# Streaming encoder step: the eight gates of the first branch ahead, its eight projections in the local attention

## Chip, core and metric

The kernel runs on one core of one Trainium2 chip. The time is what the device needs for one execution, in microseconds (us). TensorE does the matrix products; ScalarE, VectorE and GpSimd work beside it, and SyncE starts most of the DMA transfers. In the rows they are PE, ACT, DVE, POOL and SP; PEld is TensorE's loading of weights.

## What is computed

Two layers of a hybrid encoder, over 640 tokens (512 of a prompt, 128 of eight samples), width 1024. From the reference, cut:

```python
def token_mix(h, pos, lw, rel_bias, cache):
    qa, ka, va, ub, cq, ckv, kpe, ud, gate_in = split_cols(h @ lw['w_in'])
    ...   # o_a: window attention, o_b: pooling mixer, o_c: latent attention
    o_d, new_conv = conv_module(ud, conv_hist, lw['conv_w'], lw['conv_b'], lw['conv_ln_g'], lw['conv_ln_b'])
    gates = jax.nn.sigmoid(gate_in.reshape(B, T, BRANCHES, D_MODEL))
    merged = (gates[:, :, 0] * (o_a @ lw['w_o_a']) + gates[:, :, 1] * (o_b @ lw['w_o_b'])
              + gates[:, :, 2] * (o_c @ lw['w_o_c']) + gates[:, :, 3] * (o_d @ lw['w_o_d']))
    return merged @ lw['w_out'], ...
```

`conv_module` is a gated causal convolution of 31 taps, a layer norm over its 512 channels and a SiLU. After the mixers comes a feed-forward part (SwiGLU).

## The kernel before

Activations lie with the 128 features of a tile on the partitions and the 640 tokens along the free axis, in two halves of 320. Weights come in units of 128 output features: a wide unit has eight 128x128 tiles (512 KB), a projection unit four (256 KB). Each fp32 product is done in three passes over rounded parts (`w_hi*h_hi`, `w_hi*h_lo`, `w_lo*h_hi`), so one tile costs six matmuls of 320 columns: 48 for a wide unit, 24 for a projection unit.

There is no scheduler: each engine has its program written out by hand, and semaphores with counts tie them together. Units go through two slots. Unit n lies in slot n % 2 and, of the units touched here, its result in the PSUM pair `G[n % 2]`. SyncE loads `w_raw` when the unit two earlier has been split; GpSimd splits it (first the 384 columns of tiles 0 to 2, then the rest) when TensorE has finished the matching part of the unit two earlier; TensorE multiplies when it is split and when `G` has been read (`g_free`).

A layer begins with 22 wide units of the input projection. VectorE meanwhile runs the convolution. After them TensorE does small fp32 work for the branches, in the banks 4 to 7:

- `lnm`: sum over the channels of the convolution's output (L711)
- `pool` (g = 0 to 3): the pooling mixer's products (L732), each waiting for VectorE's `pooled`
- `ckvn`, `lnv`, `cqn`: sums of squares (L711) of the latent keys, of the centred convolution output and of the latent queries. ScalarE writes the squares (`squares`, L1149), then takes the root (`stds`, L1154), VectorE the reciprocal (L1613) and the scaling. From `lnv` come the layer norm, SiLU (L1310), `o_hi` (L1313) and `o_lo` (L1801), which is the input of branch D's projections; from `cqn` come the scaled queries (L1806)
- `kpe`: a product (L746) of the rotary keys `kper`, which VectorE rotates (L1814) and signals as `kpe_rot`
- transposes of new rows (`new`, `vwin`), and then the local attention, ten blocks `j`. In each, TensorE does the scores of the block after (`a_scores`), a transposition of the probabilities (`a_turn`) that VectorE has normed (`a_back`), and the values (`a_values`) after ScalarE's copy (L1359)

Between these pieces stand the 32 merges, eight of each branch in the order D, B, A, C. A merge is a gate unit from `h` in `G[0]`, its sigmoid on ScalarE into `sg` (`merge_gate`), a projection unit from `o` in `G[1]`, and the product on VectorE, which goes into `macc` (the first branch) or is added to it (`merge`). `macc` lies where `x` was; `x` is parked in HBM meanwhile. The merges of branch D were 0 and 1 before the attention, and 2 to 7 in the blocks j = 0 to 2, two in each; from j = 3 on branches B and A follow. Later, the latent attention's last part, for the samples (L978 to L998), has only one weight tile of a gate between short products.

ScalarE's functions lie in tables, and another function (root, sigmoid, SiLU, exponential) may need an ACT_TABLE_LOAD; a copy or a square needs none.

Of the kernel before, what the change touches and what calls it, by code (L numbers as in the profile page):

```python
# [16 lines left out]
ACT = mybir.ActivationFunctionType  # L17
ALU = mybir.AluOpType
# [174 lines left out]
def encoder(nc, io):  # L193
    ctx = ExitStack()
    with ctx:
# [271 lines left out]
        def a_merges(j):  # L467

            return (2 + 2 * j, 3 + 2 * j) if j < 4 else (6 + j,)
# [49 lines left out]
        def _(eng):  # L519
# [6 lines left out]
            for l in range(L):  # L526
# [64 lines left out]
        def _(eng):  # L591
            eng.sem_inc(w_split.sem, w_split.credit)
            eng.sem_inc(lo_plain.sem, lo_plain.credit)
            for l in range(L):
# [20 lines left out]
                pairs(A_UNITS // 2, M_PAIRS, UW, 4 * P)  # L615
# [9 lines left out]
        def _(eng):  # L625
# [43 lines left out]
            for l in range(L):  # L669
# [34 lines left out]

                def colsum(name, tiles, waits, square=None):
                    for n, tile in enumerate(tiles):
                        waits(n)
                        for hf, cols in halves:
                            if n == 0:
                                fill(l, (name, hf))  # L710
                            mm = eng.matmul(B[4 + hf][:, 0:HALF], ones[:, :], tile[:, cols],  # L711
                                            start=(n == 0), stop=(n == len(tiles) - 1))
                            if n == len(tiles) - 1:
                                mm.then_inc(side.sem, 1)
                        if square is not None and n < len(tiles) - 1:
                            mm.then_inc(sq_used.sem, 1)
# [31 lines left out]

                eng.wait_ge(ckv_ready.sem, ckv_ready.at(l, 1))
# [381 lines left out]
        def _(eng):  # L1131
# [42 lines left out]
            for l in range(L):  # L1174
# [100 lines left out]

                eng.wait_ge(hist_out.sem, hist_out.at(l, 16 * 4))

                for g in range(4):
                    gain = vec[:, V_PSC + g:V_PSC + g + 1]
# [8 lines left out]
                merge_gate(0)  # L1288
# [3 lines left out]
                stds(l, lambda hf: ("ckvn", hf), P)  # L1292

# [11 lines left out]
                eng.dma_start(out("o_ckv"), ckvT[:, :]).then_inc(outs.sem, 16)  # L1305

# [9 lines left out]
                merge_gate(1)  # L1316
# [31 lines left out]

                a_exps(0)
                for j in range(10):  # L1350
# [4 lines left out]
                    if n[0] == KT:  # L1355
                        branch_high(BRANCH_B, pool_out, pool_out_s)
                    merge_gate(n[0])
# [242 lines left out]
        def _(eng):  # L1600
# [33 lines left out]
            for l in range(L):  # L1634
# [141 lines left out]
                def merge(n, m, first=False):  # L1776
# [4 lines left out]

                    if not isinstance(n, int) or n:
                        eng.wait_ge(merged.sem, merged.at(l, n))
                    acc = macc[:, bass.ds(m, 1), :].rearrange("p a t -> p (a t)")
                    if first:
                        for hf, cols in halves:
                            ins = eng.tensor_tensor(acc[:, cols], sg[:, cols], G[1][:, hf, 0:HALF], ALU.mult)
                            ins.then_inc(g_free[1].sem, 1)
                        eng.wait_ge(g_free[1].sem, g_free[1].at(l, n * 2 + (A_UNITS + 2)))
                        eng.sem_inc(merged.sem, 1)  # L1790
                        return
# [16 lines left out]

                eng.wait_ge(x_parked.sem, x_parked.at(l, 16))
                merge(0, 0, first=True)  # L1810


# [5 lines left out]
                merge(1, 1, first=True)  # L1818
# [47 lines left out]
                for j in range(10):  # L1866
                    if j + 1 < 10:
                        a_front(j + 1)
                    a_back(j)
                    for n in a_merges(j):  # L1870
                        if n == KT:
                            branch_low(BRANCH_B, pool_out, pool_out_s)
                        merge(n, n % KT, first=n < KT)
# [425 lines left out]
```

## Time and profile before

| | before |
|---|---|
| median of 3 runs | 2490.18 us (2490.05 to 2490.38) |
| the profiled execution's own time | 2506.54 us |
| its span, first to last instruction | 2504.7 us |
| PE busy | 2376.0 us, 95% |
| DVE, POOL, ACT busy | 1291.9, 953.3, 860.1 us |
| mean granted TensorE clock | 0.970 |

The profiled execution took 16.36 us more than the median of the runs. Its span is 1.84 us less than its own time. A busy TensorE says nothing of its speed: the granted clock is shown apart, 1.00 for 2.4 GHz and 0.50 for 1.2 GHz.

### The profile page before, as it was taken

How to read it: one execution, taken by the hardware profiler on the slowest of the kernel's cores; microseconds unless marked ns; L12 is line 12 of the kernel's file. 1: busy time of each engine (PE TensorE's matmuls, PEld its weight loads, DVE VectorE, ACT ScalarE, POOL GpSimd, SP SyncE). 2: the span in 40 equal slices, each digit the busy share in tenths (PEclk: the TensorE clock that was granted, in tenths of full speed). 3: DMA queues.
4: the chain of work that ended last, by engine and by line, in shares of the span. 5: the costliest groups of instructions: out<-in, count | busy, mean ns of one | idle time of the engine just before them, and what ended most of it. 6: DMA issues, size and time to landing. Idle time of an engine off the chain costs nothing.

```text
span 2504.7 us, 40008 instructions
## 1 busy us (share of the span) xinstructions
PE 2376.0 (95%) x15160; PEld 2220.4 (89%) x15160; DVE 1291.9 (52%) x2296; ACT 860.1 (34%) x1688; POOL 953.3 (38%) x988
## 2 busy tenths in 40 slices
PE   6997999999999899999979989999999999999996
PEld 5996998777899899999979969987779999999996
DVE  6976243333225953826479752433332378366374
ACT  2014233334212553625410142333333145345252
POOL 3551454222166233332445415532224642423231
PEclk9999999999699999999989989999999999999998
DMA  5341121011023122222234311211012322222121
GB/s 173 113 129 52 55 73 55 26 39 39 19 97 121 51 93 70 84 92 68 69 114 139 107 32 64 68 51 38 27 38 64 113 76 75 86 76 93 61 88 55
DMA packets 70131, 186.78 MB, mean 75 GB/s; under 512 B 19648, under 2 KB 22304, under 8 KB 68960
## 3 DMA queue, kind: packets, MB, share of 16 engines
q1 hardware_dynamic: 53280, 162.23, 20.1%
q10 hardware_dynamic: 16704, 22.52, 2.7%
q8 instruction: 101, 1.65, 0.3%
q14 instruction: 46, 0.38, 0.0%
HBM read 172.41 MB, written 14.14 MB: 74 GB/s over the span
## 4 chain that ended last, share of the span: by engine, by line
PE 89%; DVE 6%; issue 2%; ACT 1%; ACTq 0%; DMA 0%; SPq 0%; DVEq 0%
PE gemm L641 44%; PE gemm L1057 16%; PE gemm L1047 13%; PE side L1057 3%; PE side L909 2%; PE side L930 2%; PE side L860 1%; DVE rstd L1613 1%; PE side L910 1%; PE side L790 1%; DVE act_lo L2038 1%; PE side L869 1%; PE side L917 1%; DVE prod L1642 1%; PE side L711 1%
## 5 line engine op out<-in xcount | busy, mean ns | idle before, releaser
L604 POOL CAST w_hi<-w_raw 128x384 fp32r<-128x384 f32 x376 | 213.0, 566 | 895.8 <-PE gemm L641 874.6
L621 POOL TENSOR_TENSOR ring_lo<-w_raw,ring_hi 128x512 fp32r<-128x512 f32 x232 | 307.9, 1330 | 590.3 <-ACT ring_hi L1475 590.3
L606 POOL TENSOR_TENSOR w_lo<-w_raw,w_hi 128x384 fp32r<-128x384 f32 x376 | 435.7, 1159 | 30.1
L641 PE MATMUL gemm<-h_hi,w_hi 128*128 128x320 f32 x1728 | 423.1, 326 | 20.1 <-DVE h_lo L1619 16.8
L641 PE MATMUL gemm<-h_lo,w_hi 128*128 128x320 f32 x1728 | 398.5, 312 | 0.0
L641 PE MATMUL gemm<-h_hi,w_lo 128*128 128x320 f32 x1728 | 398.1, 312 | 0.0
L641 PEld LDWEIGHTS gemm<-h_hi,w_hi 128*128 128x128 f32 x1728 | 290.4, 191 | 49.7 <-issue 36.3
L1057 PE MATMUL gemm<-act_hi,ring_hi 128*128 128x320 f32 x960 | 299.4, 312 | 19.0 <-issue 9.9
L1057 PE MATMUL gemm<-act_lo,ring_hi 128*128 128x320 f32 x960 | 298.7, 311 | 0.0
L1057 PE MATMUL gemm<-act_hi,ring_lo 128*128 128x320 f32 x960 | 298.4, 311 | 0.0
L641 PEld LDWEIGHTS gemm<-h_lo,w_hi 128*128 128x128 f32 x1728 | 294.1, 191 | 0.0
L641 PEld LDWEIGHTS gemm<-h_hi,w_lo 128*128 128x128 f32 x1728 | 293.1, 191 | 0.0
L1475 ACT ACTIVATE ring_hi<-w_raw 128x512 fp32r<-128x512 f32 (+1 forms) x272 | 167.6, 618 | 244.8 <-PE gemm L1047 201.7
L1793 DVE TENSOR_TENSOR prod<-gate,gemm 128x320 f32<-128x320 f32 x96 | 42.5, 484 | 326.2 <-PE gemm L641 326.2
L1057 PEld LDWEIGHTS gemm<-act_hi,ring_hi 128*128 128x128 f32 x960 | 182.2, 190 | 20.7 <-issue 20.7
L1057 PEld LDWEIGHTS gemm<-act_lo,ring_hi 128*128 128x128 f32 x960 | 182.5, 190 | 0.0
L1057 PEld LDWEIGHTS gemm<-act_hi,ring_lo 128*128 128x128 f32 x960 | 182.5, 190 | 0.0
L1696 DVE SCALAR_TENSOR_TENSOR side<-conv_prompt,vec,side 128x512 f32<-128x512 f32 x232 | 174.2, 751 | 0.0
L2115 DVE TENSOR_TENSOR x<-gemm,x 128x320 f32<-128x320 f32 x96 | 42.7, 486 | 224.6 <-PE gemm L1047 224.6
L1047 PE MATMUL gemm<-hu_hi,ring_hi 128*128 128x320 f32 x640 | 146.1, 309 | 0.0
L1047 PE MATMUL gemm<-hu_hi,ring_lo 128*128 128x320 f32 x640 | 145.8, 309 | 0.0
L1047 PE MATMUL gemm<-hu_lo,ring_hi 128*128 128x320 f32 x640 | 145.7, 309 | 0.0
(280 smaller groups left out, 4247.0 us busy)
## 6 DMA issues: line engine op xcount, KB each, us to landing
w_raw<-in_ws_ff SPq DMA_DIRECT2D x120, 512.0 KB, 3.2
w_raw<-in_ws_gate SPq DMA_DIRECT2D x64, 512.0 KB, 3.3
w_raw<-in_ws_in SPq DMA_DIRECT2D x44, 512.0 KB, 3.3
w_raw<-in_ws_proj SPq DMA_DIRECT2D x64, 256.0 KB, 2.6
w_raw<-in_ws_out SPq DMA_DIRECT2D x16, 512.0 KB, 3.3
w_raw<-in_ws_fd SPq DMA_DIRECT2D x16, 384.0 KB, 3.0
x_park<-x ACTq DMA_DIRECT2D x2, 2560.0 KB, 12.1
x<-x_park ACTq DMA_DIRECT2D x4, 1280.0 KB, 5.8
```

The costliest lines, as they stand in the source:

```text
L604: eng.tensor_copy(w_hi[s][:, cols], w_raw[s][:, cols]).then_inc(w_high.sem, 1)
L606: eng.tensor_tensor(w_lo[s][:, cols], w_raw[s][:, cols], w_hi[s][:, cols].bitcast(F32), ALU.subtract).then_inc(w_split.sem, 1)
L621: eng.tensor_tensor(lo, src, hi.bitcast(F32), ALU.subtract).then_inc(lo_plain.sem, 1)
L641: mm = eng.matmul(dst[:, hf, 0:HALF], w, r[:, k, cols], start=first and k == 0 and part == 0, stop=last and k == kk - 1 and part == 2)
L909: eng.matmul(bank[:, 0:w], qh[h % 2][:, P * i:w], kh[h % 2][:, 0:w], start=True, stop=False)
L930: mm = eng.matmul(B[6][part, i * P:(i + 1) * P], v_tok[k][:, 64 * h:64 * h + 64], PT[i % 2][:, k * P:(k + 1) * P], start=(k == 0), stop=(k ...
L1047: mm = eng.matmul(dst[:, hf, 0:HALF], w[:, cut], r[:, cols], start=part == 0 and k == 0 and t == 0, stop=part == 1 and k == tiles - 1 and ...
L1057: mm = eng.matmul(dst, w[:, cut], r[act][:, k, :], start=fresh and k == 0 and t == 0, stop=k == 3 and t == 2, skip_group_check=not fresh)
L1475: eng.activation(hi, src, ACT.Copy).then_inc(op_high.sem, 1)
L1696: eng.scalar_tensor_tensor(acc, src, w, acc, ALU.mult, ALU.add).then_inc(conv_step.sem, 1)
L1793: eng.tensor_tensor(t2[0][:, cols], sg[:, cols], G[1][:, hf, 0:HALF], ALU.mult)\
L2115: eng.tensor_tensor(x[:, m, cols], G[u % 2][:, hf, 0:HALF], x[:, m, cols], ALU.add)\
```

## The change

Branch D's eight gate units come first, one after the other: gate 0 behind `lnm`, gates 1 and 2 in halves behind the four pooling products, gate 3 behind `ckvn`, 4 behind `lnv`, 5 behind `cqn`, 6 behind `kpe`, 7 behind the transposes. ScalarE writes each sigmoid straight into `macc`. The eight projection units then stand in the attention: 0 to 2 in block 0, 3 to 5 in block 1, 6 and 7 in block 2; VectorE multiplies `macc` by each in place. The other branches are as they were. Since both kinds of unit now come in runs, gate m and projection m lie in slot and `G` m % 2. The loads and the splits follow that order. The core of the diff:

```diff
         def a_merges(j):
-            return (2 + 2 * j, 3 + 2 * j) if j < 4 else (6 + j,)
+            return () if j < 3 else ((KT, KT + 1) if j == 3 else (KT - 2 + j,))
+        def a_projections(j):
+            return range(3 * j, min(3 * j + 3, KT)) if j < 3 else ()
...
+                with eng.Fori(0, KT // 2) as i:
+                    for s in range(2):
+                        unit(i * 2 + (A_UNITS + s), s, layer_of(io["ws_gate"], l * M_PAIRS + i * 2 + s), UW)
+                with eng.Fori(0, KT // 2) as i:
+                    for s in range(2):
+                        unit(i * 2 + (A_UNITS + KT + s), s, layer_of(io["ws_proj"], l * M_PAIRS + i * 2 + s), 4 * P)
...
-                merge_units(0, KT + 5)
+                merge_units(KT, KT + 5)
...
+                def first_gate(m, first=0, last=KT):
+                    if first == 0:
+                        psum(m % 2, A_UNITS // 2 + m // 2)
+                    for t in range(first, last):
+                        product(l, A_UNITS + m, G[m % 2], m % 2, t, KT, h_hi, h_lo)
+                def first_projection(m):
+                    psum(m % 2, A_UNITS // 2 + KT // 2 + m // 2)
+                    for t in range(4):
+                        if m == 0:
+                            eng.wait_ge(o_split.sem, o_split.at(l, t + 1))
+                        product(l, A_UNITS + KT + m, G[m % 2], m % 2, t, 4, o_hi, o_lo)
...
+                first_gate(0)
                 for g in range(4):
...
-                    merge_tiles(0, 2 * g, 2 * g + 2)
+                    first_gate(1 + g // 2, 4 * (g % 2), 4 * (g % 2) + 4)
                 colsum("ckvn", *sq_tiles(0, 1), square=True)
+                first_gate(3)
                 colsum("lnv", *sq_tiles(1, 4), square=True)
+                first_gate(4)
                 colsum("cqn", *sq_tiles(5, 2), square=True)
-                merge_tiles(0, 8, 12)
-                merge_tiles(1, 0, 12)
-                eng.wait_ge(loaded, 16 * 5)
+                first_gate(5)
                 eng.wait_ge(kpe_rot.sem, kpe_rot.at(l, 1))
...
+                first_gate(6)
                 eng.wait_ge(ckv_ready.sem, ckv_ready.at(l, 1))
...
+                first_gate(7)
                 a_scores(0)
...
-                    merge_tiles(n[0], 0, 8)
+                    for m in a_projections(j)[:2]:
+                        first_projection(m)
+                    if n:
+                        merge_tiles(n[0], 0, 8)
                     a_turn(j)
-                    merge_tiles(n[0], 8, 12)
+                    for m in a_projections(j)[2:]:
+                        first_projection(m)
+                    if n:
+                        merge_tiles(n[0], 8, 12)
                     a_values(j)
```

On ScalarE:

```diff
+                def first_gate(m):
+                    eng.wait_ge(unit_done.sem, unit_done.at(l, A_UNITS + m + 1))
+                    for hf, cols in halves:
+                        eng.activation(macc[:, m, cols], G[m % 2][:, hf, 0:HALF], ACT.Sigmoid)\
+                           .then_inc(g_free[m % 2].sem, 1)
```

On VectorE:

```diff
-                eng.wait_ge(x_parked.sem, x_parked.at(l, 16))
-                merge(0, 0, first=True)
...
-                merge(1, 1, first=True)
+                def first_merge(m):
+                    eng.wait_ge(unit_done.sem, unit_done.at(l, A_UNITS + KT + m + 1))
+                    for hf, cols in halves:
+                        eng.tensor_tensor(macc[:, m, cols], macc[:, m, cols], G[m % 2][:, hf, 0:HALF], ALU.mult)\
+                           .then_inc(g_free[m % 2].sem, 1)
...
                     a_back(j)
+                    for m in a_projections(j):
+                        first_merge(m)
```

On TensorE, around `kpe` in the first layer, before (the last tile of merge 1's projection, the two products, the first transposes):

```order
L641 MATMUL gemm<-o_hi,w_hi_57 128x320
L641 MATMUL gemm<-o_lo,w_hi_57 128x320 x2
L641 MATMUL gemm<-o_hi,w_lo_58 128x320 x2
L746 MATMUL side<-kpe_raw,dup 128x320 [waits side_read6,kpe_rotated,consts_loaded]
L746 MATMUL side<-kpe_raw,dup 128x320 [waits side_read7]
L756 MATMUL side<-ident,ckv 16x128 [waits side_read5,gemm_read1,ckv_ready]
L757 MATMUL side<-ident,v_window 16x128
```

The same place now (the last tile of gate 5, the two products, the first of gate 6):

```order
L653 MATMUL gemm<-h_hi,w_hi_57 128x320 x2
L653 MATMUL gemm<-h_lo,w_hi_57 128x320 x2
L653 MATMUL gemm<-h_hi,w_lo_58 128x320 x2
L773 MATMUL side<-kpe_raw,dup 128x320 [waits side_read6,kpe_rotated]
L773 MATMUL side<-kpe_raw,dup 128x320 [waits side_read7]
L653 MATMUL gemm<-h_hi,w_hi_53 128x320 [waits w_split,gemm_read0]
L653 MATMUL gemm<-h_hi,w_hi_53 128x320
```

The product stays where it was among the small ones, but a gate instead of merge 0's projection and merge 1 stands between `cqn` and it, and a gate behind it. On ScalarE, between the layer norm's root and the squares of `cq`, before:

```order
L1154 ACTIVATE rstd<-side,eps 128x320 [waits side_filled,ckv_ready]
L1154 ACTIVATE rstd<-side,eps 128x320 [waits side_filled]
L1305 DMA o_ckv<-ckv 128x640
L1149 ACTIVATE square_77<-cq 128x640 [waits gemm_read0]
L1149 ACTIVATE square_76<-cq 128x640 [waits gemm_read1]
L1310 ACT_TABLE_LOAD
L1310 ACTIVATE conv_out<-conv_out,vec 128x640 [waits ln_scaled]
```

and now:

```order
L1189 ACT_TABLE_LOAD [waits side_filled]
L1189 ACTIVATE rstd<-side,eps 128x320 [waits ckv_ready]
L1189 ACTIVATE rstd<-side,eps 128x320 [waits side_filled]
L1353 DMA o_ckv<-ckv 128x640
L1315 ACT_TABLE_LOAD
L1315 ACTIVATE x<-gemm 128x320 [waits unit_done]
L1315 ACTIVATE x<-gemm 128x320
L1184 ACTIVATE square_77<-cq 128x640 [waits gemm_read0]
L1184 ACTIVATE square_76<-cq 128x640 [waits gemm_read1]
L1359 ACT_TABLE_LOAD
L1359 ACTIVATE conv_out<-conv_out,vec 128x640 [waits ln_scaled]
```

Gate 4's sigmoid (into `x`, that is `macc`) with a table load stands ahead of the squares, so they and the SiLU wait for gate 4's unit.

## Rows read from the trace of the kernel before

**Rows 1.** Windows: us, busy of PE, PEld, DVE, ACT, POOL, clock, DMA share, GB/s

```profile
185.12:325.27 140.15, 125.42 (x739) 110.82 (x737) 59.24 (x100) 48.80 (x86) 48.96 (x66) 0.94 0.18 56
1427.53:1567.67 140.14, 125.40 (x738) 110.81 (x736) 59.34 (x100) 48.85 (x86) 48.98 (x66) 0.94 0.19 56
```

**Rows 2.** PE's waits between 180 and 262 us: total, times, longest

```profile
PE gemm L641 <- issue: 5.3, 1, 5.3
PE side L711 <- ACT square L1149: 4.6, 3, 1.6
PE side L732 <- DVE rstd L1746: 2.7, 2, 2.2
PE side L790 <- ACT v_sample L1329: 1.4, 1, 1.4
```

**Rows 3.** Timeline of PE: start, us, what, idle before

```profile
216.35 2.42 PE L711 MATMUL side<-square,ones 128*128 128x320 f32 x8 [1.56 <-ACT square L1149]
...
224.06 0.87 PE L641 MATMUL gemm<-o_hi,w_hi 128*128 128x320 f32 x2 [5.30 <-issue]
```

**Rows 4.** Windows of 4 us around the longest wait, columns as in rows 1

```profile
218.00:222.00 4.00, 0.77 (x3) 0.19 (x1) 3.96 (x4) 1.31 (x3) 0.00 (x0) 0.92 0.00 0
222.00:226.00 4.00, 1.94 (x7) 1.97 (x8) 3.30 (x5) 3.94 (x6) 0.00 (x0) 0.50 0.00 0
```

**Rows 5.** The chain, in order of time, in attention block 1

```profile
277.29 7.24 PE gemm L641 x48
...
284.96 3.52 PE gemm L641 x24
```

**Rows 6.** Timeline of ACT, sigmoid of gate 0 to the root of `cqn`

```profile
205.86 0.77 ACT L1266 ACTIVATE gate<-gemm 128x320 f32<-128x320 f32 x2 [1.08 <-PE gemm L641]
...
215.56 1.36 ACT L1149 ACTIVATE square<-cq 128x640 f32<-128x640 f32 x2
216.94 1.28 ACT L1310 ACT_TABLE_LOAD   x1
220.88 0.83 ACT L1310 ACTIVATE conv_out<-conv_out,vec 128x640 f32<-128x640 f32 x1 [2.66 <-DVE conv_out L1765]
...
226.95 1.28 ACT L1154 ACT_TABLE_LOAD   x1
228.25 0.95 ACT L1154 ACTIVATE rstd<-side,eps 128x320 f32<-128x320 f32 x2
...
285.21 0.60 ACT L1359 ACTIVATE rstd<-side 128x512 f32<-128x512 f32 x1
```

**Rows 7.** Timeline of DVE: queries, rotation, and block 2's front to block 1's norm

```profile
229.29 4.15 DVE L1613 RECIPROCAL rstd<-rstd 128x640 f32<-128x640 f32 x1 [1.50 <-ACT rstd L1154]
233.48 2.11 DVE L1806 SCALAR_TENSOR_TENSOR cq<-cq,vec,rstd 128x640 f32<-128x640 f32 x2
...
236.52 0.82 DVE L1814 TENSOR_TENSOR kpe_raw<-kpe_raw,cos_sin 64x640 f32<-64x640 f32 x1
...
277.32 0.69 DVE L1833 SCALAR_TENSOR_TENSOR square<-side,bias_prompt 128x512 f32<-128x512 f32 x1 [0.58 <-PE side L790]
...
281.06 1.39 DVE L1862 TENSOR_TENSOR square<-square,softmax_stats 128x512 f32<-128x512 f32 x1
```

**Rows 8.** Windows: latent attention of the samples, both layers, columns as in rows 1

```profile
617.16:671.26 54.10, 50.52 (x197) 40.91 (x197) 9.33 (x38) 13.72 (x48) 6.00 (x8) 0.56 0.08 25
...
1859.50:1895.40 35.90, 32.31 (x196) 25.71 (x195) 9.33 (x38) 13.72 (x48) 6.00 (x8) 0.98 0.12 37
```

**Rows 9.** Timeline of POOL: one wide unit's split, in the input projection

```profile
178.41 0.72 POOL L604 CAST w_hi<-w_raw 128x640 fp32r<-128x640 f32 x1 [2.56 <-PE gemm L641]
179.21 1.58 POOL L606 TENSOR_TENSOR w_lo<-w_raw,w_hi 128x640 fp32r<-128x640 f32 x1
181.05 0.50 POOL L604 CAST w_hi<-w_raw 128x384 fp32r<-128x384 f32 x1 [0.27 <-PE gemm L641]
181.63 1.02 POOL L606 TENSOR_TENSOR w_lo<-w_raw,w_hi 128x384 fp32r<-128x384 f32 x1
```

More of the change, by code:

```diff
@@ L614, in _ @@
                 pairs(0, A_UNITS // 2, UW, UW)
-                pairs(A_UNITS // 2, M_PAIRS, UW, 4 * P)
+                pairs(A_UNITS // 2, KT // 2, UW, UW)
+                pairs(A_UNITS // 2 + KT // 2, KT // 2, 4 * P, 4 * P)
+                pairs(A_UNITS // 2 + KT, M_PAIRS - KT, UW, 4 * P)
                 pairs(A_UNITS // 2 + M_PAIRS, KT // 2, UW, UW)
@@ L1273, in branch_high @@
                         eng.activation(o_hi[:, t, NP:T], sample(t), ACT.Copy).then_inc(o_high.sem, 1)
+                def first_gate(m):
[3 more added lines that the diff above has]
+                           .then_inc(g_free[m % 2].sem, 1)
+                eng.wait_ge(x_parked.sem, x_parked.at(l, 16))
+                first_gate(0)
                 eng.wait_ge(hist_out.sem, hist_out.at(l, 16 * 4))
                 for g in range(4):
+                    if g == 2:
+                        first_gate(1)
                     gain = vec[:, V_PSC + g:V_PSC + g + 1]
@@ L1286, in _ @@
                        .then_inc(freed(("pool", g, 1)), 1)
-                merge_gate(0)
+                first_gate(2)
                 eng.wait_ge(pooled.sem, pooled.at(l, 4))
@@ L1292, in _ @@
                 stds(l, lambda hf: ("ckvn", hf), P)
+                first_gate(3)
                 def centred(k):
@@ L1305, in _ @@
                 eng.dma_start(out("o_ckv"), ckvT[:, :]).then_inc(outs.sem, 16)
+                first_gate(4)
                 squares(l, 2, lambda k: cq[:, k, :], 5, lambda k: read_unit(eng, l, 14 + k))
@@ L1315, in _ @@
                 stds(l, lambda hf: ("cqn", hf), 2 * P)
-                merge_gate(1)
+                first_gate(5)
+                first_gate(6)
                 for hf, cols in halves:
@@ L1347, in a_exps @@
                     eng.activation(stat(j, 4), stat(j, 4), ACT.Exp).then_inc(a_esink.sem, 1)
+                first_gate(7)
                 a_exps(0)
@@ L1354, in _ @@
                     n = a_merges(j)
-                    if n[0] == KT:
+                    if j == 3:
                         branch_high(BRANCH_B, pool_out, pool_out_s)
-                    merge_gate(n[0])
+                    if n:
+                        merge_gate(n[0])
                     bank = filled(eng, l, ("At", j))
@@ L1774, in branch_low, with merge @@
                            .then_inc(o_split.sem, 1)
-                def merge(n, m, first=False):
+                def merge(n, m):
                     eng.wait_ge(unit_done.sem, unit_done.at(l, n * 2 + (A_UNITS + 2)))
                     eng.wait_ge(g_free[0].sem, g_free[0].at(l, n * 2 + (A_UNITS + 2)))
-                    if not isinstance(n, int) or n:
-                        eng.wait_ge(merged.sem, merged.at(l, n))
+                    eng.wait_ge(merged.sem, merged.at(l, n))
                     acc = macc[:, bass.ds(m, 1), :].rearrange("p a t -> p (a t)")
[L1785 to L1791, printed above, removed]
                     for hf, cols in halves:
@@ L1817, in _ @@
                 eng.memset(mask_q[:, 0:CHUNK], 1.0).then_inc(masks.sem, 1)
-                merge(1, 1, first=True)
+                def first_merge(m):
[3 more added lines that the diff above has]
+                           .then_inc(g_free[m % 2].sem, 1)
+                    eng.wait_ge(g_free[m % 2].sem, g_free[m % 2].at(l, 2 * (A_UNITS // 2 + KT // 2 + m // 2) + 2))
+                    eng.sem_inc(merged.sem, 1)
                 def a_front(j):
@@ L1872, in _ @@
                             branch_low(BRANCH_B, pool_out, pool_out_s)
-                        merge(n, n % KT, first=n < KT)
+                        merge(n, n % KT)
                 branch_low(BRANCH_A, window_out, window_out_s)
```

## The prediction

> **What bounds the kernel now.** I read the page first: TensorE is busy for 95% of the span, so matrix work sets most of the time and only two things can be won, its waits and its half-speed stretches. Then the windows by stage. The change touches the stretch from `lnm` to branch B's first gate; it takes 140.15 us in the first layer and 140.14 in the second, and TensorE is busy for only 125.4 of them, at a mean granted clock of 0.94 [rows 1]. The reader should see that the two layers are the same, so one timeline does for both. Next the list of TensorE's waits there: 5.3 once, 4.6 in three times, 2.7 in two and 1.4 once, together 14.0 us [rows 2]. The timeline says what each is. The 5.3 stands before the first `gemm<-o_hi`: merge 0's projection waits for the layer norm, SiLU and the split of the convolution's output [rows 3]. The list calls it "issue", but the instruction behind it reads `o_hi` and `o_lo`. The 4.6 are the waits for ScalarE's squares, one each for `ckvn`, `lnv` and `cqn`, the last 1.56 [rows 2, 3]. The 2.7 are pooling products that wait for VectorE, the 1.4 the first scores, which wait for ScalarE to clear the last transposes [rows 2].
>
> Then the clock. A mean of 0.94 over 140.15 us is about 17 us at 1.2 GHz (0.06 x 2 x 140.15) [rows 1]. Around the longest wait it falls shortly before 222 (0.92 in one window, 0.50 in the next) [rows 4]; the work resumes at 224.06 [rows 3], so some 2.7 us of the 17 lie in the wait and cost nothing. In the other 14 TensorE works at half speed and loses 7.0 us. So one layer's stretch holds 119.1 us of work at full speed and 21.0 us of loss. The work stays: the same tiles are multiplied. Nothing before or behind the stretch is moved.
>
> **The change, part by part.** Gate units: 7.24 us each behind a small product [rows 5], 7.04 of it (48/24 of the 3.52 that a projection unit takes [rows 5]) for the matmuls alone. They need only `h` and weights.
>
> *Pooling waits, 2.7 us.* Each pooling product now has half a gate, 3.5 us, behind it instead of two tiles, 1.8 us. The wait in question was at most 2.2 us long [rows 2] with 1.8 us of cover, so VectorE needs no more than 4.0 us between two products plus what ScalarE adds. But it computes its levels without waiting for TensorE, and only the last step, about 1.3 us, needs the product before. Gate 0, another 7 us, has let it get ahead. I take all 2.7 off. ScalarE's new sigmoids, 0.77 [rows 6], stand before the copies that free banks; half a gate covers them.
>
> *Squares, 4.6 us.* They stay. In the new order `ckvn`, `lnv` and `cqn` each stand right behind a gate, and on ScalarE the squares stand behind that gate's sigmoid, as `ckv`'s square did before. Sigmoid 0.77 and one square, half of 1.36 [rows 6], make 1.45; the three old waits average 1.53 [rows 2]. I keep 4.6.
>
> *The 5.3 us.* Branch D's projections now stand in the attention, over 30 us later. Gone.
>
> *The 1.4 us before the scores.* Gate 7, 7 us, covers ScalarE's copies. Gone.
>
> *The new wait.* `kpe` needs `kpe_rot`, and VectorE's rotation stands behind the norm of `cq`. Before, two projections and a gate ran in between and nobody waited for it. Take the end of gate 4 as zero. ScalarE: sigmoid and two squares of `cq`, 0.77 + 1.36, with their overlap until 2.05; table load 1.28, until 3.35; from the first SiLU to the next table load 226.95 - 220.88 = 6.07, until 9.4; that load and the root, 226.95 to 229.20, until 11.7 [rows 6]. The 2.66 us for which ScalarE waited before the first SiLU [rows 6] are gone: the layer norm's root, reciprocal and scaling (1.28 + 0.95, 4.15, about 3.3) start when `lnv` ends, a gate earlier, at -7.1, and end at 2.6. VectorE: reciprocal and scaling, 229.29 to 235.59, 6.3, until 18.1; rotation 0.82, until 18.9 [rows 7]. TensorE: wait 1.5, `cqn` 2.42 [rows 3], gate 5 7.1, done at 11.0. So it waits 7.9 us, in each layer. Queued behind it are gate 6, which needs nothing of it, and the transposes. This takes back more than the 5.3 gave.
>
> *Table loads.* Between the sigmoids stand new loads. Those for gates 3 and 4 lie under gates; the two on the path just worked out are in its sum at 1.28 us, as the row shows. The load begins at 216.94, when the squares end at 216.92, so nothing lies ahead of it [rows 6].
> The Trainium skill (ScalarE: Activation LUTs, "What ACT_TABLE_LOAD costs") counts about 2.66 us for every switch, a load of 1.28 and a drain of 1.38. By it, with the drain beside a load already in the row, the wait would be 10.7 us instead of 7.9, and the whole time 5.5 us longer than my sum; this trace agrees with the load and shows no drain.
>
> *Projections in the attention.* In block 1 TensorE has two projections, 7.04 us, between the scores and the turn; VectorE needs from 277.32 to 282.45, 5.1 us, for the front of one block and the norm of the other [rows 7], and 0.9 for a product that frees `G`. Covered, by 1 us. Block 2 has no third projection, so its values stand right behind the turn and wait for ScalarE's copy, 0.60 [rows 6], with its start about 0.9 us. A bound: 0.6 to 1.1.
>
> *Weights.* GpSimd's split of a wide unit is 0.72 + 1.58 + 0.50 + 1.02 = 3.82 us [rows 9] against 7.04 of TensorE. A projection unit has 1.52 of it for the first three tiles and a fourth tile, bounded by nothing and by the 2.30 of five tiles [rows 9]: 1.5 to 3.8 us against 3.52. At the upper end it costs 0.3 a unit, 2.4 a layer; by columns it is near 2.0 and costs nothing, which I take.
>
> *Clock.* No row shows the new order, so two bounds. Below: nothing is lost. Above: 7.0 us as now. Of the three old half-speed stretches the first followed a pooling wait, the last the transposes and the 1.4 us; both causes go, gates follow at once. After the 7.9 us wait I expect what followed the 5.3: work resumed at 224.06 and reached full speed near 228.3, 4.3 us at half speed, 2.2 lost.
>
> Sum for a layer: 4.6 + 7.9 + 0.9 + 2.2 = 15.6 us of loss for 21.0, a gain of 5.4; for two 10.8. Against the profiled execution's own 2506.54 us that is 2495.7. But this execution is no plain copy of the timed runs. In the first layer the samples' attention, the same instructions, took 54.10 us at a clock of 0.56, in the second 35.90 at 0.98 [rows 8]: 18.2 us. Without that the execution would have its own time at 2488.3, close to the median of 2490.18 and 1.8 below; so the timed runs, alike within 0.33 us, seem free of it. The gain is taken off the median: 2490.2 - 10.8 = **2479.4 us**.
>
> **Rivals.**
> *A. The clock falls as much as now.* The squares' waits break the gates and the new wait is longer than the old. Then 13.4 + 7.0 = 20.4 us for 21.0: 1.2 us gained, 2489.0, the same within what counts. For it: the old pooling wait of 2.2 us was followed by half speed. Against it: dense units between the waits. Chance 0.12. Partial forms lie between 2480 and 2489.
>
> *B. The samples' attention falls to half speed in the timed runs.* Everything behind the stretch starts 5 us earlier in layer one and 11 in layer two, and that stage, one tile of a gate between short fp32 products, is where the clock fell in one layer of two. Its price, 18.2 us [rows 8], is more than the gain: 2497.6, slower. It decides as soon as one layer has it in most runs. Against it: three timed runs of the old kernel do not show it. Chance 0.11.
>
> *C. The table switch costs its drain.* The mechanism here would be an idle gap of 1.4 us by each of two loads on the path to `kpe_rot`, in both layers, against the 0.02 us between square and load that the row shows. 2484.9, chance 0.03.
> It is the rule of the Trainium skill's page ScalarE: Activation LUTs that is weighed above.
>
> *D. The gates hide nothing more than they did:* the wait moves whole, that is the `kpe` wait is longer than the waits removed. From 5.3 + 2.7 + 1.4 = 9.4 us saved, 8.8 are given back (7.9 + 0.9). So without the clock almost nothing is won: 0.6 a layer. That is A seen from the waits, 2489.0, and its chance is in A's 0.12. My forecast hangs on the half-speed stretches, 4.8 of the 5.4 us.
>
> **How the numbers follow.** My own case, chance 0.74, runs from 2475.0 (no half speed: 7.6 us a layer) to about 2486 (a clock loss of 5). With C it is faster, 0.77. A gives the same, 0.12; B slower, 0.11. 0.2%, some 5 us, is about what a measurement of this kernel can tell from no change. The range 2473 to 2491 takes in my case, A and C with a little beyond the best, and leaves out B.
>
> **What the changed kernel's profile would show.** No wait before a `gemm<-o_hi` of branch D and none at the first scores. One wait of about 8 us at the `kpe` products, released by VectorE's rotation, in both layers. Three waits of 1.5 us for squares. From `lnm` to branch B's first gate 134.7 us by my sum, 132.5 if nothing runs at half speed; a mean clock there of 0.96 or more. Attention blocks 0 to 2 without a wait but the 0.9 us. I am wrong if GpSimd's splits or VectorE's products of the projections make TensorE wait in blocks 0 to 2, if the clock stays down for more than some 5 us, or if the samples' attention takes near 54 us in the runs that are timed.

## The result, and the profile after

The change made the kernel slower. This kernel's median is 2507.07 us over 20 runs (2488.64 to 3339.57), that of before is 2492.07 over 20 (2490.05 to 2531.13), the three runs of the table ahead of the prediction among them. The ratio is 1.0048, 95% interval 1.0026 to 1.0071: 0.48% slower, where 0.4% faster was forecast. The run of 3339.57 us, at a mean clock of 0.65, is left out below.

A median hides here what the single runs show. Each kernel's times fall into levels 15 to 21 us apart, and the profiles, which caught runs on all three, say what a level is: the number of layers in which the samples' latent attention ran at half speed. A run without a profile is put on a level by its time. Over this comparison and those of the experiments the old kernel had 119 runs, the new one 31:

| runs (median, us) | no layer | one layer | two layers |
|---|---|---|---|
| before, 119 runs | 66 (2491.5) | 39 (2508.8) | 14 (2529.5) |
| after, 31 runs | 1 (2488.6) | 22 (2506.7) | 8 (2521.6) |

Level by level the new kernel is 2 to 8 us faster. It is slower because 30 of its 31 runs have at least one such layer, and of the old kernel's 53 of 119.

The profiled execution of after took 2504.89 us, with this span and clock (a digit for each fortieth of the span):

```profile
span 2503.0 us, 39978 instructions
...
PEclk9999999999999899999999999999978999999998
```

The 7 and 8 at three quarters of the span are the samples' attention of layer 2. Windows over that stage in both layers and, above them, from `lnm` to branch B's first gate (us, busy of PE, PEld, DVE, ACT, POOL, clock, DMA share, GB/s), the stretches of [rows 1] and [rows 8]:

```profile
185.54:325.35 139.81, 123.26 (x738) 109.13 (x736) 65.59 (x100) 44.89 (x83) 51.71 (x66) 0.95 0.19 55
1409.62:1547.79 138.17, 121.62 (x740) 107.79 (x738) 65.57 (x100) 44.88 (x83) 51.72 (x66) 0.96 0.19 56
617.24:653.41 36.17, 32.59 (x198) 26.02 (x197) 9.33 (x38) 13.70 (x48) 6.00 (x8) 0.97 0.12 37
1839.67:1893.96 54.29, 50.70 (x198) 41.23 (x197) 9.34 (x38) 13.70 (x48) 5.99 (x8) 0.56 0.08 25
```

Two things are to be read. The changed stretch, 140.15 and 140.14 us before [rows 1], is now 139.81 and 138.17: a gain of 0.34 + 1.97 = 2.3 us, by one execution of each, where 10.8 were forecast. And the stage that wasn't touched costs 54.29 - 36.17 = 18.1 us more in layer 2 than in layer 1, as it did in layer 1 of before [rows 8]. The two profiled executions have one such layer each, so their difference, 2506.54 to 2504.89, tells nothing of the loss in the medians.

TensorE's waits between 183 and 330 us (total, times, longest), to be laid beside [rows 2]:

```profile
PE side L773 <- DVE kpe_raw L1853: 7.5, 1, 7.5
PE side L738 <- ACT square L1184: 4.4, 3, 1.5
PE side L760 <- DVE rstd L1798: 3.2, 1, 3.2
PE side L848 <- ACT prod L1411: 0.7, 1, 0.7
```

They sum to 15.8 us, before to 14.0. Layer 2 has the same four. The waits of 5.3 and 1.4 us are gone, the one for `kpe_rot` has come, and the pooling wait, of which nothing was to be left, has grown. With the prediction's estimate of 119.1 us of work, 139.81 - 119.1 - 15.8 = 4.9 us went to half speed in layer 1 and 3.3 in layer 2. The chain of after shows where, first a pooling product and its half gate in layer 1 and in layer 2, then the `kpe` product and gate 6 in layer 1 (start, us):

```profile
214.00 1.97 PE side L760 x4
215.97 4.49 PE gemm L653 x24
...
1438.43 1.34 PE side L760 x4
1439.77 3.54 PE gemm L653 x24
...
261.86 2.50 PE side L773 x4
264.36 9.43 PE gemm L653 x48
```

The same product and half gate take 6.46 us in layer 1 and 4.88 in layer 2: 1.6 us of half speed behind the pooling wait. A gate is 7.04 us [rows 5] and took 9.43, and `kpe` 2.50 instead of about 1.3: 3.6 us of half speed behind the new wait. Windows of 4 us, ahead of the end of that wait and behind it, show the clock:

```profile
256.00:260.00 4.00, 0.00 (x0) 0.00 (x0) 3.96 (x2) 1.17 (x3) 0.84 (x1) 0.87 0.18 66
...
264.00:268.00 4.00, 4.00 (x15) 3.71 (x15) 0.00 (x0) 0.00 (x0) 0.00 (x0) 0.50 0.00 0
```

### The profile page after: what moved, and what is told of

Read it like the earlier page. It is cut to its first block, busy times and chain, and to the rows that moved or that the text cites. A ratio compares the mean times of both kernels' runs of the same rounds, so it can differ in the third digit from the quotient of the medians.

```text
span 2503.0 us, 39978 instructions
## 1 busy us (share of the span) xinstructions
PE 2370.0 (95%) x15160; PEld 2215.4 (89%) x15160; DVE 1307.1 (52%) x2296; ACT 851.9 (34%) x1682; POOL 957.3 (38%) x988
## 4 chain that ended last, share of the span: by engine, by line
PE 89%; DVE 7%; ACT 2%; issue 2%; ACTq 0%; DMA 0%; SPq 0%; DVEq 0%
PE gemm L653 43%; PE gemm L1092 16%; PE gemm L1082 13%; PE side L1092 3%; PE side L944 2%; PE side L965 2%; PE side L895 1%; DVE rstd L1665 1%; PE side L945 1%; DVE act_lo L2087 1%; PE side L738 1%; PE side L818 1%; PE side L904 1%; PE side L952 1%; DVE prod L1694 1%
```

## The experiments

Three questions: do the half-speed layers make the loss (the first seven runs), what do the two waits cost (three), and is a version to be had that beats both (two). In the diffs `-` and `+` are against the changed kernel unless it is said.

### Is the loss in the levels, and does the start time move them?

My theory: what decides is when the samples' attention starts. Its start in layer 1 is the same in both kernels, 617.16 and 617.24 us [rows 8]. In layer 2 it starts at 1839.67 now; before it was 1859.50 [rows 8], less the 18.2 that the half-speed layer had added 1841.3. So the new kernel is 1.6 us earlier there. The rival: the levels are luck of the day, and the new kernel has its share of runs without a fall like the old.

The first run gives those 1.6 us back with work that nobody needs: in layer 2, eleven products into `G[0]`, whose result the gate behind them overwrites, ahead of merge 11. (Merge 11 is the fourth of branch B, in attention block 5; the text put on record ahead of the run calls it branch A's gate.)

```
                         if t % KT == 0:
                             psum(t // KT, n + A_UNITS // 2)
+                        if n == 11 and t == 0 and l in (1,):
+                            eng.wait_ge(w_split.sem, w_split.at(l, unit * 2 + 1))
+                            for _ in range(11):
+                                eng.matmul(G[0][:, 0, 0:HALF], w_hi[0][:, 0:P], h_hi[:, 0, 0:HALF],
+                                           start=True, stop=True)
```

> The changed kernel with 11 extra matmuls of 320 columns (h_hi by a weight tile that is loaded, their result overwritten) ahead of branch A's gate 11 in the second layer alone: 1.6 us of delay for everything behind, nothing else changed. Theory S (start time): whether the samples' attention falls to half speed is set by the time at which it starts, to about a us; the new order made it start 1.6 us sooner in the second layer than an undisturbed run of the old kernel does (1839.7 against 1859.5 - 18.2 = 1841.3), and at the same time in the first. Then the delay takes most of the falls away: median about 2490.2 (2488.6 + 1.6). Rival T (the order itself, or what it leaves behind, makes the fall likely): 1.6 us do nothing, median about 2508.7. Rival N (pure chance for each run): a mixture as before, most runs at 2507.

12 runs, median 2506.17: five without a half-speed layer (2488.3 to 2491.1), five with one, two with two. Ratio to before 1.0013 (0.9975 to 1.0050). With more work five runs of twelve are on a level that the kernel without it reached once in 31; but the median of 2490.2 that my theory gave didn't come. The same was then tried on the kernel before (twelve products, layer 2), where a theory of start times wants a clear change: eight runs of 12 with none, four with one, median 2493.73, ratio 0.9998 (0.9964 to 1.0032). Beside it the plain old kernel had 17 of 35 with none; twelve runs can't tell that from no change.

The changed kernel again, unchanged:

> The changed kernel itself once more, beside fresh runs of the old one. Level theory: each kernel has levels some 17.5 us apart, by how many of its two layers fall to half speed in the samples' attention (old 2490.5, 2508.5, 2530; new 2488.6, 2506.5, 2522), and which level a run takes is decided outside the kernel, differently from job to job. Then both kernels take all levels, in like shares, and level by level the new one is 2 us faster. Order theory: the new order makes the fall likely; at least 9 of 12 runs at 2505 or above, against half or fewer of the old kernel's.

12 runs, median 2506.95, ratio 1.0053 (1.0013 to 1.0093): none without, seven with one, five with two. The rival falls: the old kernel beside it had 17 of 29 without. This run's profile has its half-speed layer in layer 1, whose start the change hardly moved. So the 1.6 us in layer 2 can't be the whole reason. Nor does the start alone, to half a us, tell the outcome. The first score product of layer 1, in this execution and in that of after:

```profile
619.79 0.38 PE L1013 MATMUL side<-ckv_cache_t,q_latent_sample 128*128 128x128 f32 x2
```

```profile
620.25 0.38 PE L1013 MATMUL side<-ckv_cache_t,q_latent_sample 128*128 128x128 f32 x2
```

The same kernel, 0.46 us apart at this point, is at half speed in that stage the first time and at full speed the second.

The first run again, and the same products in layer 1 instead of 2 (`l in (0,)`):

> The same kernel as e1 once more: the changed kernel with 1.6 us of extra matmuls in the second layer alone, ahead of branch A's gate 11. In e1 5 of 12 runs had no fall to half speed in the samples' attention, in the changed kernel itself 1 of 31. If the start time of the stage matters: again 4 to 8 of 12 runs at 2488 to 2492. If e1 was chance: at most one.

> The changed kernel with the same 1.6 us in the first layer alone; both layers' stages then start 1.6 us later. If the start time matters for each layer, the shares change here too, and differently from e1 and e9, where only the second was moved: I expect 3 to 8 of 12 runs without a fall. If only the distance between the two layers' stages matters, it is as in the changed kernel: at most one.

With the shift in layer 2: median 2506.13, three without, six with one, three with two; ratio 1.0005 (0.9970 to 1.0040). That is under the four to eight that I expected, but with the first run 8 of 24 against 1 of 31. With the shift in layer 1: median 2490.78, seven without, four with one, one with two; ratio 0.9995 (0.9955 to 1.0035). So 1.6 us of useless work in layer 1 bring the median back by 16 us; in layer 2 they leave it where it was. That such work changes the share is shown: the old kernel beside these runs kept its usual one (17 of 35 and 14 of 24 without). That it does so by the start time is the likely reading, and isn't shown. Against a simple rule speaks that two edits below, gate 6 ahead of `kpe` and gate 2 whole, start the samples' attention earlier by 6 to 20 us in their traces and leave the share as it was: 2 and 0 runs of 12 without.

### What if the stage is made denser?

In the samples' attention a tile of merge 24's gate, the first of branch C, is multiplied for each sample, the first of them behind the scores of two samples. Now each tile stands one sample earlier, the first ahead of the loop behind the first scores, and the last sample has none. In all nine half-speed stages that the profiles caught, the clock falls 3.1 to 4.2 us behind the first score product; now one dense tile lies ahead of that place and one on it. First on the kernel before, then on the changed one:

```
                 s_scores(0)
+                merge_tiles(3 * KT, 0, 1)
                 for b in range(NB):
...
-                    merge_tiles(3 * KT, b, b + 1)
+                    if b + 1 < NB:
+                        merge_tiles(3 * KT, b + 1, b + 2)
```

> The kernel before the change; in the samples' attention the first weight tile of the gate stands between the scores of sample 0 and 1 (before: behind both), every later tile one sample earlier, none at sample 7. Nothing is added or left out. In all falls and most no-falls seen, the clock falls 3.3 to 4.1 us behind the stage's first product or not at all, so what TensorE does in the first 4 us of the stage would decide. If that is so: with two tiles of dense work there and no wait, no run falls: all at 2490 to 2494. If the whole stage is too thin and the first 4 us are not special: the falls come at other places, as often.

> The changed kernel with the same shift of the gate's tiles. If the start of the stage decides: all runs at 2488 to 2492, the changed kernel's lowest level, and about 2 us under the old kernel with the same shift. If not: levels as in the changed kernel itself.

Before with it: all 12 runs between 2489.2 and 2495.2, median 2492.41, ratio 0.9958 (0.9920 to 0.9996). After with it: all 12 between 2485.1 and 2491.3, median 2487.43, ratio 0.9949 (0.9915 to 0.9983). Windows of the latter over the stage in both layers:

```profile
616.97:653.18 36.21, 32.58 (x197) 25.97 (x197) 9.80 (x38) 13.73 (x48) 6.01 (x8) 0.98 0.12 37
...
1839.71:1875.92 36.21, 32.58 (x196) 25.93 (x197) 9.81 (x38) 13.72 (x48) 6.01 (x8) 1.00 0.12 37
```

Full speed in both, in 36.21 us, while the start in layer 2 is the same 1839.7 as in the profile of after. Eight tiles, each moved by one sample, make the new kernel 19.5 us faster than itself (2487.43 to 2506.95) and faster than the old one. It settles the sign: without the half-speed layers the change is worth 2492.41 - 2487.43 = 5.0 us, and the loss comes whole from the stage that it doesn't touch. The stretch from `lnm` to branch B's first gate explains these 5.0 us, in both layers, first in the old order with the moved tiles, then in the new:

```profile
185.90:328.04 142.14, 125.80 (x739) 111.45 (x737) 59.55 (x100) 48.80 (x86) 49.59 (x66) 0.94 0.19 55
1413.12:1553.58 140.46, 125.70 (x739) 111.33 (x737) 59.54 (x100) 48.86 (x86) 48.98 (x66) 0.94 0.19 55
```

```profile
185.42:325.32 139.90, 123.37 (x739) 109.28 (x737) 65.58 (x100) 44.91 (x83) 51.79 (x66) 0.95 0.19 55
1409.83:1547.76 137.93, 121.40 (x739) 107.56 (x737) 65.56 (x100) 44.91 (x83) 51.79 (x66) 0.96 0.19 56
```

282.6 against 277.8 us is 4.8 of the 5.0. The 2.3 us read further up are smaller because the old order's stretch isn't the same in every execution: its layer 1 took 140.15 us in the profile of before and 142.14 here, where the pooling waits are 4.4 us instead of 2.7.

### What do the new waits cost?

`kpe`: gate 6 ahead of the product that waits.

```
                 first_gate(5)
+                first_gate(6)

                 eng.wait_ge(kpe_rot.sem, kpe_rot.at(l, 1))
...
-                first_gate(6)
                 eng.wait_ge(ckv_ready.sem, ckv_ready.at(l, 1))
```

> The changed kernel with gate 6 ahead of the kpe product instead of behind it. The wait for the rotation was 7.5 us, and behind it TensorE worked 7.3 us at half speed (3.6 lost). If the wait is the step that took the gain back: gate 6 covers 7.0 of it, at most 0.5 is left, the half-speed piece goes; 10.6 us a layer, 21 in all: 2467.5 in runs without a fall in the samples' attention, 2485.7 with one. If TensorE meets another wait in its place (the transposes behind it need banks that ScalarE clears after gate 6's sigmoid): less than 10 in all.

12 runs, median 2485.27: eight between 2483.2 and 2487.6, the level with one half-speed layer, two above (2502.5 and 2504.5, two layers by the profile of the former), two below (2462.96 and 2470.04). Ratio 0.9941 (0.9910 to 0.9971). Level by level 21.4 us under the changed kernel, for the level with one. Waits between 183 and 340 us, and the clock behind:

```profile
PE side L760 <- DVE rstd L1798: 3.2, 1, 3.2
...
PE side L774 <- DVE kpe_raw L1853: 0.5, 1, 0.5
```

```profile
260.00:280.00 20.00, 19.23 (x124) 15.03 (x124) 4.82 (x13) 7.67 (x16) 3.11 (x6) 1.00 0.11 31
```

The wait is down from 7.5 to 0.5 us and the half speed behind it is gone, clock 1.00. Two waits of 7.0 less, and half speed of 3.6 us in layer 1 and 3.2 in layer 2 (gate 6 took 9.04 us there), make 20.8 of the 21.4 measured. A gate's order, nothing else.

Pooling: all of gate 2 between the third and the fourth pooling product, and none of it behind the fourth.

```
-                    first_gate(1 + g // 2, 4 * (g % 2), 4 * (g % 2) + 4)
+                    if g < 2:
+                        first_gate(1, 4 * g, 4 * g + 4)
+                    elif g == 2:
+                        first_gate(2)
```

> The changed kernel with all of gate 2 between the pooling products 2 and 3, none behind 3. The wait for pooled of group 3 was 3.2 us in both layers, and in the first the clock fell with it (1.6 lost). If the cover was too short: 7.0 us hide it all, 3.2 in both and 1.6 in one layer, 8 us in all: 2480.6 without a fall in the samples' attention, 2498.8 with one. If VectorE's adds are slowed further because GpSimd's splits come at other times (adds of 0.70 took 1.96 where a split ran beside them): 1 to 3 us a layer less.

12 runs, median 2499.84: eight at 2495.7 to 2500.1 (one layer; the profile has it in layer 1), four at 2514.9 to 2518.2; ratio 1.0035 (1.0003 to 1.0066). The level with one is 8.7 us under the changed kernel's, the level with two 5.3. In its list of waits the pooling line is gone and the squares have 5.0 us for 4.4. Of 12 runs none is without a half-speed layer, so starting the later stages some us earlier doesn't by itself change the level.

What had lengthened VectorE's way to the last `pooled` from 5.4 us before (197.3 to 202.7) to 8.0? VectorE's timeline of after, between `pooled` 3 and 4 (start, us, what):

```profile
205.84 0.70 DVE L1776 TENSOR_TENSOR square<-pool_prompt 128x526 f32<-128x526 f32 x1
206.45 0.92 DVE L1778 TENSOR_TENSOR prod<-pool_sample 128x240 f32<-128x240 f32 x1
207.40 1.96 DVE L1776 TENSOR_TENSOR square<-square 128x524 f32<-128x524 f32 x1
...
209.70 0.70 DVE L1776 TENSOR_TENSOR square<-square 128x520 f32<-128x520 f32 x1
...
211.02 1.37 DVE L1776 TENSOR_TENSOR square<-square 128x512 f32<-128x512 f32 x1
```

And GpSimd's in the same time:

```profile
206.24 0.87 POOL L614 CAST w_hi<-w_raw 128x640 fp32r<-128x640 f32 x1 [3.54 <-PE gemm L653]
207.19 1.62 POOL L616 TENSOR_TENSOR w_lo<-w_raw,w_hi 128x640 fp32r<-128x640 f32 x1
210.13 0.64 POOL L614 CAST w_hi<-w_raw 128x384 fp32r<-128x384 f32 x1 [1.32 <-PE gemm L653]
210.85 0.99 POOL L616 TENSOR_TENSOR w_lo<-w_raw,w_hi 128x384 fp32r<-128x384 f32 x1
```

Four adds of `square`, of one kind and nearly one size: 0.70 us where they lie almost wholly ahead of GpSimd's work, 1.96 and 1.37 where its subtraction runs. The smaller add of `prod` begins under the cast and takes 0.92 us. In the test's trace below, with nothing of GpSimd beside it, it takes 0.40, so the casts slow VectorE too. The Trainium skill (SBUF — State Buffer, "Who interferes with whom") says that a `tensor_tensor` of VectorE with both inputs in SBUF contends with GpSimd's reads; the rows agree. The 640 columns are the second part of gate 3's unit, the 384 the first part of gate 4's. The test, on the kernel with the moved tiles, holds the whole split of gate 3's unit until the last `pooled`, and with it all that GpSimd does behind it:

```
-                def split(pair, s, width):
+                def split(pair, s, width, held=False):
...
+                        if held and not part:
+                            eng.wait_ge(pooled.sem, pooled.at(l, 4))
                         done = unit_done if part else part_done
...
-                pairs(A_UNITS // 2, KT // 2, UW, UW)
+                pairs(A_UNITS // 2, 1, UW, UW)
+                split(A_UNITS // 2 + 1, 0, UW)
+                split(A_UNITS // 2 + 1, 1, UW, held=True)
+                pairs(A_UNITS // 2 + 2, KT // 2 - 2, UW, UW)
```

> e7 (the changed kernel with the tiles of the samples' attention shifted, which keeps all runs at one level, median 2487.4) with GpSimd's split of gate 3's unit held back until the last pooled: the unit is needed some 5 us later still, and nothing else moves. If VectorE's adds were slowed by the splits beside them (1.96 for 0.70), the chain between two pooled falls from 8.0 to 5.4 us, the wait before pooling product 3 from 3.2 to about 0.6, and the half-speed piece behind it goes where it was: 5 to 7 us less, 2481 to 2482. If VectorE is slow there for another reason: 2487 as before, or more, if gate 3's split is now late.

Seven runs, all between 2475.6 and 2479.6, median 2477.36, ratio 0.9923 (0.9894 to 0.9952): 10.1 us under the kernel with the moved tiles alone, more than the 5 to 7 expected. VectorE's adds in its trace, and GpSimd's next piece:

```profile
205.68 0.40 DVE L1785 TENSOR_TENSOR prod<-pool_sample 128x240 f32<-128x240 f32 x1
206.12 0.70 DVE L1783 TENSOR_TENSOR square<-square 128x524 f32<-128x524 f32 x1
...
208.16 0.69 DVE L1783 TENSOR_TENSOR square<-square 128x512 f32<-128x512 f32 x1
```

```profile
210.56 0.50 POOL L616 CAST w_hi<-w_raw 128x384 fp32r<-128x384 f32 x1 [10.91 <-DVE rstd L1805]
```

The way from `pooled` 3 to 4 is 5.4 us again and TensorE doesn't wait there. Two layers of 3.2 and the 1.6 of half speed make 8.0 of the 10.1. Another 1.4 lie in gate 6 behind the `kpe` wait: it takes 8.37 and 8.71 us here, 9.45 and 9.07 with the moved tiles alone. That leaves 0.7.

### All together

The moved tiles, gate 6 ahead of `kpe`, and gate 2 whole; then the same with the held split in place of the whole gate 2.

> The changed kernel with three steps at once: gate 6 ahead of the kpe product, all of gate 2 between the pooling products 2 and 3, and the shift of the tiles in the samples' attention. The first took 21 us off each level, the second 9. If the three don't touch one another and the third keeps the clock up: all runs at 2458 to 2461. If the third does nothing: 2458, 2476 and 2494.

> The changed kernel with gate 6 ahead of the kpe product, the split of gate 3's unit held back until the last pooled, and the shifted tiles in the samples' attention. If the three are independent: e11's 2477.4 less the 21 us of the first step, 2456, all runs at one level, 3 us under e8. If holding back the split and whole gate 2 were the same gain by two ways: 2459, as e8.

Six runs each. The first 2458.0 to 2460.1, median 2459.18, ratio 0.9826 (0.9763 to 0.9888). The second 2457.2 to 2459.9, median 2459.43, ratio 0.9828 (0.9798 to 0.9859). By the medians the two cures of the pooling wait are worth the same. Had the three steps been independent, the second would be some 3 us better, near 2456. Its trace shows where these 3 us are. The stretch takes 248.4 us in the two layers together, that of the first 251.5; but they are lost again behind the samples' attention. The 20 us that begin 30 us behind its first score product, in both layers, in the first kernel and in the second:

```profile
636.58:656.58 20.00, 17.34 (x114) 17.13 (x111) 6.72 (x14) 8.43 (x16) 8.10 (x11) 0.91 0.16 45
1845.58:1865.58 20.00, 17.34 (x114) 17.13 (x111) 6.86 (x14) 8.43 (x16) 8.27 (x11) 0.91 0.16 46
```

```profile
634.57:654.57 20.00, 17.34 (x103) 16.97 (x100) 5.92 (x12) 8.43 (x16) 6.50 (x8) 0.75 0.12 38
1844.80:1864.80 20.00, 17.34 (x110) 17.13 (x106) 6.19 (x13) 8.43 (x16) 7.59 (x10) 0.83 0.13 39
```

TensorE is shown busy for the same 17.34 us and does less, at a clock of 0.75 and 0.83 instead of 0.91. This is one execution of each. All waits of the second in the stretch:

```profile
PE side L743 <- ACT square L1191: 4.4, 3, 1.5
...
PE side L853 <- ACT prod L1418: 0.7, 1, 0.7
...
PE side L779 <- DVE kpe_raw L1860: 0.5, 1, 0.5
```

5.6 us, where before had 14.0 [rows 2]. So the idea of the change holds: in this order it makes the kernel 1.7% faster. The median is about 33 us under the old kernel's 2492.07, and 48 us lie between the change as it was made and the same change with three edits. In all kernels with the moved tiles together, 43 runs, not one had a half-speed layer.

## Why the prediction was wrong

**The step that failed** is Rival B's dismissal: "Against it: three timed runs of the old kernel do not show it", chance 0.11. I had the stage, its price (18.2 us, measured 18.1) and the sign. Its time of 2497.6 was still 9.5 us under the measured 2507.07, since it counted on a gain of 10.8, and its reason, a stage that starts 5 and 11 us earlier, didn't come: in the profile the stage starts 0.1 us later in layer 1 and 1.6 earlier in layer 2. I had seen that of the two layers of one profiled execution one had it. Against that stood three runs alike. But by the counts now known the old kernel is without it in 66 of 119 runs, so three in a row without happen by luck in one case of six (0.55 cubed). Three runs can't tell "free of it" from "in every second run", and the one execution that could be looked into had it. The step "so the timed runs, alike within 0.33 us, seem free of it" took a median for a property of the kernel. What a shift by a few us does to such a stage wasn't to be foreseen in direction; that its share might change either way was.

**The waits, one by one.** The new `kpe` wait was worked out at 7.9 us and is 7.5, in both layers. The three squares 4.6, measured 4.4. Block 2's values 0.9, measured 0.7. The 5.3 and the 1.4 are gone as said. GpSimd's splits in blocks 0 to 2 make nobody wait, and the table load on the way to the root of `cq` is 1.28 us with nothing between it and the instruction ahead, so Rival C didn't come.

**"I take all 2.7 off"** is the mis-sized term: a wait of 3.2 us stands in its place, 3.2 a layer off. The old wait and its cover gave VectorE's way rightly: 4.0 us and the product's own 1.3 are within 0.1 of the 5.4 of before, and the product with half a gate, 4.9, would have left 0.5. But the new order puts a wide unit's split beside that way, and it takes 8.0. I had costed such a split (3.82 us against 7.04 of TensorE) for who waits for it, not for whose adds it slows. Holding one split shows it: adds back at 0.70 us, the wait gone.

**"4.3 us at half speed, 2.2 lost"** is the second: behind the `kpe` wait half speed lasted into gate 6, 3.6 and 3.2 us lost, and in layer 1 the pooling wait, which I had dropped, cost 1.6 more. By what is left of the stretch when work and waits are taken off, together 4.9 and 3.3 for 2.2.

**The sum.** Waits 15.8 for 13.4, half speed 4.1 on the mean for 2.2: 19.9 us of loss for 15.6, a gain of 1.15 us a layer for 5.4. By this pair of profiles the change is 2.3 us better, by the kernels with moved tiles 5.0, nearer to Rival A's 1.2 than to my 10.8. That Rival A comes near is in part luck: it kept 7.0 us of half speed and 13.4 of waits, while half speed fell to 4.1 and the waits rose to 15.8. With so little won, Rival B decides the sign. (The upper end of my own case, "about 2486" at a clock loss of 5, is 2485.0 by its own terms; nothing hangs on it.)

**What stays open.** Why the new order falls in nearly every run and the old in fewer than half. Shown are that 1.6 us of useless work ahead of the stage change the share (8 of 24 and 7 of 12 runs without, against 1 of 31), that it isn't the start in layer 2 alone, since layer 1 has it too, and that the dense tiles one sample earlier end it. The Trainium skill (TensorE: Matmul & The Clock Gate, "What's actually happening") has the monitor run free of the kernel's start, so that the moment at which the clock changes depends on where a run happens to meet it. The spread over one kernel's runs fits that, but no run here can set where it meets it.

## What to carry to other kernels

If the trace shows a stage at half clock in one layer and at full clock in its twin, count that stage as a coin whose odds a change elsewhere may move, price it first (here 18 us against a gain of 5), and make it dense before anything else is judged. Don't conclude from three equal times that it is gone. When work of one engine is moved beside work of another, look also at whose instructions it slows: here GpSimd's splits beside VectorE's adds cost TensorE 3.2 us a layer. And a wait that the sum foresees, as the 7.5 us at `kpe`, is best moved behind the next independent gate before the kernel is timed: that alone was 21 us.

## What the runs showed of the hardware

The samples' attention of layer 2 in after's trace, windows around the fall and around the recovery, then TensorE's products at the fall:

```profile
1840.00:1844.00 4.00, 4.00 (x28) 3.37 (x26) 1.08 (x3) 0.59 (x1) 2.25 (x4) 1.00 0.39 131
1844.00:1848.00 4.00, 3.49 (x19) 2.62 (x18) 1.83 (x7) 2.65 (x7) 0.00 (x0) 0.77 0.19 66
1884.00:1888.00 4.00, 4.00 (x14) 3.33 (x14) 0.00 (x0) 0.98 (x4) 1.86 (x2) 0.50 0.00 0
...
1896.00:1900.00 4.00, 4.00 (x25) 4.00 (x25) 0.81 (x4) 1.15 (x3) 1.38 (x2) 0.83 0.02 4
```

```profile
1845.94 0.55 PE L653 MATMUL gemm<-h_lo,w_hi 128*128 128x320 f32 x2
1846.29 0.73 PE L653 MATMUL gemm<-h_hi,w_lo 128*128 128x320 f32 x2
...
1847.96 0.79 PE L1013 MATMUL side<-ckv_cache_t,q_latent_sample 128*128 128x128 f32 x2 [0.51 <-ACT prod L1486]
```

I had expected half speed only behind a wait. Here the clock goes from 2.4 to 1.2 GHz, in the middle of a tile (0.55 us for two products, then 0.73), while the profile has TensorE busy without a gap, mostly with small fp32 products; the 0.51 us that are missing in the second window come behind the fall. It stays down although TensorE is shown busy for 50.70 of the 54.29 us, until the dense products behind the stage. The busy share of the page doesn't tell a stretch that keeps the clock from one that doesn't; only the granted clock does. Second, one VectorE add of 524 columns takes 0.70 us alone and 1.96 beside GpSimd's subtraction of 640, and one of 240 columns 0.40 alone and 0.92 beside a cast. Third, a TensorE wait of 7.5 us cost 11.1: 3.6 more of half speed behind it.
